# 1/rms of a stage's input norm multiplied in behind the products, on an eight-stage kernel

## The reference

```python
def rms_norm(x, g):
    y = x * lax.rsqrt(jnp.mean(x * x, axis=-1, keepdims=True) + EPS)
    return y * g
mixer_a: u, v, z = split(h @ w_in); v = rms_norm(v, v_gain); mixed = causal w_s over chunks of 128 (v) + b_s
         y = u * mixed * silu(z);  return y @ w_out
mixer_b: q, k, v for 3 dilated window patterns x 8 heads: rms_norm of q and k, rotary, windowed softmax, merge of the three
         y = o * silu(z);  return y @ w_out
mixer_c: xc, z = split(h @ w_in); pooled = causal means of xc over 2, 4, 8, 16
         y = ((pooled - xc) @ w_grp) * scale * silu(z);  return y @ w_out
swiglu:  (silu(h @ w_gate) * (h @ w_up)) @ w_down
even mixer: differential attention (4 heads) | u * sigmoid(gate) -> causal convolution of 31 taps -> layernorm -> silu;  @ w_out
odd mixer:  S5 state space recurrence on 256 channels | latent attention (6 heads) with norms of both latents;  @ w_out
```

## Time and profile before

| what | value |
|---|---|
| median of 3 runs | 3223.59 us (3222.73 to 3223.64) |
| profiled execution, span | 3221.1 us |
| PE busy | 3003.4 us, 93% |
| DVE busy | 1588.9 us, 49% |
| ACT busy | 1105.8 us, 34% |
| POOL busy | 322.8 us, 10% |

### The profile page before, as it was taken

How to read it: one execution, slowest core, us unless ns; L and a number is a source line. 1 busy time by engine, 2 the same in 40 slices (tenths; PEclk the granted TensorE clock), 3 DMA queues, 4 the chain that set the end, 5 groups by cost and what they waited for, 6 DMA issues and landing times.

```text
span 3221.1 us, 37674 instructions
## 1 busy us (share of the span) xinstructions
PE 3003.4 (93%) x13472; PEld 2403.3 (75%) x13472; DVE 1588.9 (49%) x2188; ACT 1105.8 (34%) x1575; POOL 322.8 (10%) x281
## 2 busy tenths in 40 slices
PE   7999999998999899998999988689999888889998
PEld 6888787877788777776888866467888654668886
DVE  5444444553355454454444487844333578453333
ACT  3332223452344432223332244434222333442222
POOL 1000001100111000000000042210000443000001
PEclk9999999999999999999999988789999898999999
DMA  3222221112111122222222221012222210112222
GB/s 137 99 91 91 99 92 59 53 53 73 66 59 53 59 93 91 86 92 79 92 91 93 90 79 53 20 67 86 97 98 98 81 51 13 59 63 100 92 97 85
DMA packets 69245, 252.04 MB, mean 78 GB/s; under 512 B 7680, under 2 KB 7680, under 8 KB 68480
## 3 DMA queue, kind: packets, MB, share of 16 engines
q1 hardware_dynamic: 66960, 241.89, 22.2%
q10 hardware_dynamic: 2160, 8.49, 0.7%
HBM read 248.25 MB, written 2.10 MB: 78 GB/s over the span
## 4 chain that ended last, share of the span: by engine, by line
PE 81%; DVE 11%; issue 3%; ACT 3%; POOL 2%; DMA 0%; ACTq 0%; POOLq 0%; DVEq 0%
PE ps L276 18%; PE ps L278 18%; PE ps L277 18%; PE ps L492 2%; PE ps L493 2%; PE ps L494 2%; DVE arena L1549 2%; PE ps L702 1%; PE ps L665 1%; PE ps L666 1%; PE ps L667 1%; PE ps L712 1%; PE ps L692 1%; PE ps L510 1%; PE ps L1002 1%
## 5 line engine op out<-in xcount | busy, mean ns | idle before, releaser
L265 DVE TENSOR_TENSOR w_low<-raw,w_high 128x1024 fp32r<-128x1024 f32 x456 | 577.5, 1269 | 533.9 <-ACT w_high L258 524.8
L276 PE MATMUL ps<-h_high,w_high 128*128 128x512 f32 x1968 | 785.4, 399 | 27.9 <-DVE h_low L379 26.0
L277 PE MATMUL ps<-h_low,w_high 128*128 128x512 f32 x1968 | 772.6, 393 | 0.0
L278 PE MATMUL ps<-h_high,w_low 128*128 128x512 f32 x1968 | 772.1, 392 | 0.0
L258 ACT ACTIVATE w_high<-raw 128x1024 fp32r<-128x1024 f32 x456 | 478.0, 1052 | 467.9 <-PE ps L278 233.9
L276 PEld LDWEIGHTS ps<-h_high,w_high 128*128 128x128 f32 x1968 | 372.6, 189 | 121.6 <-issue 32.1
L278 PEld LDWEIGHTS ps<-h_high,w_low 128*128 128x128 f32 x1968 | 372.9, 189 | 78.4
L277 PEld LDWEIGHTS ps<-h_low,w_high 128*128 128x128 f32 x1968 | 373.4, 190 | 74.5 <-issue 1.4
L276 PE MATMUL ps<-y_high,w_high 128*128 128x512 f32 x800 | 313.9, 392 | 0.5 <-DVE y_low L1456 0.4
L277 PE MATMUL ps<-y_low,w_high 128*128 128x512 f32 x800 | 312.7, 391 | 0.0
L278 PE MATMUL ps<-y_high,w_low 128*128 128x512 f32 x800 | 312.5, 391 | 0.0
(11 more groups left out here) (343 smaller groups left out, 3950.7 us busy)
## 6 DMA issues: line engine op xcount, KB each, us to landing
raw<-stream SPq DMA_DIRECT2D x456, 512.0 KB, 3.2
table<-tables_in ACTq DMA_DIRECT2D x5, 1088.0 KB, 5.0
x<-x_in ACTq DMA_DIRECT2D x8, 256.0 KB, 8.2
x_out<-x SPq DMA_DIRECT2D x8, 256.0 KB, 2.0
const<-const_in SPq DMA_DIRECT2D x1, 673.0 KB, 4.9
work<-ssm_in ACTq DMA_DIRECT2D x1, 512.0 KB, 3.7
params<-params_in ACTq DMA_DIRECT2D x1, 287.0 KB, 8.6
```

Source lines behind the costliest of these rows:

```text
L265: nc.vector.tensor_tensor(w_low[:, u.slot], raw[:, u.raw], w_high[:, u.slot].bitcast(F32), ALU.subtract).then_inc(weights_low, 1)
L276: nc.tensor.matmul(bank, wh, high[:, k], start=k == 0, stop=False)
L277: nc.tensor.matmul(bank, wh, low[:, k], start=False, stop=False)
L278: mm = nc.tensor.matmul(bank, wl, high[:, k], start=False, stop=k == tiles - 1)
```

## The change

The split input of a stage no longer holds 1/rms: `h_high` and `h_low` are the split of x * gain. They are made tile by tile by `high_of` (ACT) and `low_of` (DVE) as the output products of the stage before are added to x (argument `following`), or in the post norm's pass. The column sums stand behind the first unit of the next stage (in b ahead of its first product), the spread in the middle of its second (`mid`), and ACT copies 1/rms to SBUF (`late_keep`). In b it is spread near the end of each half. Wherever a product leaves PSUM, DVE multiplies it by 1/rms: u, z in a; x tiles and z in c; gate and up in f; gates, and the rotary tables, in e; the inputs of the recurrence and the rotary key in o; v and z in b. So silu and sigmoid read SBUF behind that multiply, and PE's waits for a bank are for DVE's take (`c_z_taken`, `f_gate_taken`, `b_z_taken`) and no longer for ACT. The epsilons of inner norms are scaled (`norm_eps`, `b_args`, `o_args`). In the post norm's pass DVE adds all tiles; POOL adds the squares, as for the other norms, and the sums by ones and the reciprocal of a full tile are gone. `normalise()` goes. At the start the raw loads are issued ahead of const, and params right behind the first x tile.

```diff
+        def high_of(act, name, k):
+            xk, gain, high, _ = h_tile(name, k)
+            nc.scalar.activation(high, xk, ACT.Copy, scale=gain).then_inc(h_high_done, 1)
+        def low_of(dve, name, k):
+            xk, gain, high, low = h_tile(name, k)
+            dve.wait_ge(h_high_done, 8 * H_NO[name] + k + 1)
+            nc.vector.scalar_tensor_tensor(out=low, in0=xk, scalar=gain, in1=high.bitcast(F32), op0=ALU.mult,
+                                           op1=ALU.subtract).then_inc(h_low_done, 1)
+        def norm_sums(pe, r, classes=False):
+            if r > 0:
+                pe.wait_ge(norm_added, r)
+            pe.wait_ge(norm_gathered, 6 * (r + 1))
+            column_sums(root, 0, classes).then_inc(norm_summed, 1)
+            pe.wait_ge(norm_squared, 8 * (r + 1))
+            column_sums(ssq, 1, classes).then_inc(norm_summed, 1)
+        def late_keep(act, name, bank, target):
+            act.wait_ge(late_spread, S_NO[name] + 1)
+            nc.scalar.activation(target, ps[:, bank], ACT.Copy).then_inc(late_kept, 1)
...
                     u = Unit(first + at + j, loop, per)
                     split_low(dve, u + AHEAD)
+                    if following is not None and at + j > 0:
+                        low_of(dve, following, at + j - 1)
                     dve.wait_ge(units_done, u.count(1))
...
         def b_tensor(pe, t, first, o, y_base, r, last=False, following=None):
             pe.wait_ge(out_free, 8 * o + 2)
+            norm_sums(pe, R_PRE["b"], True)
...
+                    if (j, u) == (BH, 1):
+                        pe.wait_ge(b_k_done, lin(3 * BH, i, 3 * BH))
+                        norm_spread(pe, R_PRE["b"], 3).then_inc(b_r_spread, 1)
...
-                            pe.wait_ge(b_silu, lin(u - 1, i, BH))
+                            pe.wait_ge(b_z_taken, lin(u - 1, i, BH))
                         product(pe, unit, ps[:, n % 2], h_high, h_low)
...
-                    if j == BH and u < 3:
-                        dve.wait_ge(b_o_copied, lin(u + 1, i, 3))
-                        gate(u, b_o[:, u])
+                    if j == BH and 1 <= u <= BH:
+                        m = u - 1
+                        dve.wait_ge(b_r_kept, lin(1, i, 1))
+                        dve.wait_ge(units_done, b_unit(first, i, BH, m).count(1))
+                        nc.vector.tensor_tensor(b_szs[m % 2][:], ps[:, m % 2], b_r[:], ALU.mult).then_inc(b_z_taken, 1)
+                        if m < BH - 1:
+                            dve.wait_ge(b_o_copied, lin(m + 1, i, 3))
+                            gate(m, b_o[:, m])
...
             for k in range(KD):
                 if k >= 2:
-                    dve.wait_ge(*post_done(p, k - 2))
+                    dve.wait_ge(post_added, 8 * p + k - 1)
                 nc.vector.scalar_tensor_tensor(out=full[:, k % 2], in0=source[:, k], scalar=par(gain, k), in1=ps[:, 7],
                                                op0=ALU.mult, op1=ALU.mult).then_inc(post_scaled, 1)
-                if k % 2:
+                if k >= 1:
                     add(k - 1)
+                if k >= 2 and following is not None:
+                    low_of(dve, following, k - 2)
...
                     split_low(dve, Unit(plan[g][0] + m + AHEAD))
+                    if g == 0 and m == 0:
+                        norm_rstd(dve, R_PRE["c"])
+                        dve.wait_ge(late_kept, S_NO["c"] + 1)
                     dve.wait_ge(units_done, plan[g][0] + m + 1)
...
+                    nc.vector.tensor_tensor(c_x[:, b], ps[:, m], rstd[:], ALU.mult).then_inc(c_pool, 1)
...
+                    dve.wait_ge(units_done, plan[g][1] + m + 1)
+                    nc.vector.tensor_tensor(c_sz[:, m], ps[:, 4 + m % 2], rstd[:], ALU.mult).then_inc(c_z_taken, 1)
...
+                if slot > 0 and e_unit(slot - 1)[1] == "b" and slot % 2 == 0:
+                    m = e_unit(slot - 1)[2]
+                    dve.wait_ge(e_sig, m + 1)
+                    dve.wait_ge(e_taken, e_takes(m) + 2)
+                    nc.vector.tensor_tensor(e_u[:, m, PADT:], e_u[:, m, PADT:], e_sg[m % 2][:], ALU.mult).then_inc(e_gated, 1)
...
-            pool.wait_ge(rstd_spread, R_PRE["o"] + 1)
+            pool.wait_ge(norm_summed, 2 * (R_PRE["o"] + 1))
             nc.gpsimd.tensor_copy(o_eb, early).then_inc(o_small_done, 1)
...
-            sp.dma_start(const[:], const_in).then_inc(const_loaded, 16)
             for s in range(RAW_SLOTS):
                 sp.dma_start(raw[:, s], stream[s]).then_inc(weights_loaded[s], 16)
+            sp.dma_start(const[:], const_in).then_inc(const_loaded, 16)
```

More of the change, by code:

```diff
@@ L266, in split_low, with product @@
                                     ALU.subtract).then_inc(weights_low, 1)
-        def product(pe, u, bank, high, low, ready=None, tiles=KD):
+        def product(pe, u, bank, high, low, ready=None, tiles=KD, mid=None):
             pe.wait_ge(weights_low, u.count(1))
             for k in range(tiles):
+                if mid is not None and k == tiles // 2:
+                    mid()
                 if ready is not None:
@@ new lines, in norm_sums, with norm_spread @@
+        def norm_sums(pe, r, classes=False):
[5 more added lines that the diff above has]
+            column_sums(ssq, 1, classes).then_inc(norm_summed, 1)
+        def norm_spread(pe, r, bank):
+            pe.wait_ge(rstd_done, r + 1)
+            for b in range(NBLK):
+                mm = nc.tensor.matmul(ps[:, bank, b * P:(b + 1) * P], norm_rstds[:, b:b + 1].to_broadcast([P, P]), ident,
@@ L349, in norm_rstd @@
[L349 to L364 removed]
+            act.wait_ge(norm_added, r + 1)
@@ L409, in rounds, with out_product @@
                     body(i, 0)
-        def out_product(pe, o, first, y_base, tiles=KD, r=None, last=False):
+        def out_product(pe, o, first, y_base, tiles=KD, r=None, last=False, following=None):
             def body(loop, at):
@@ L419, in out_product, with out_split @@
             rounds(pe, last, body)
-            if r is not None:
-                norm_sum(pe, r)
-        def out_split(act, o, first, target=None, r=None, last=False):
+            if r is not None and following is None:
+                norm_sums(pe, r)
+                norm_spread(pe, r, 7).then_inc(rstd_spread, 1)
+        def out_split(act, o, first, target=None, r=None, last=False, following=None):
             def body(loop, at):
@@ L512, in a_tensor, with a_scalar @@
                         mm.then_inc(mix_done, 1)
[L513 to L515 removed]
+                out_product(pe, o + half, start + 16, y_base + 8 * half, r=r if half == 1 else None, last=last and half == 1,
+                            following=following)
+        def a_scalar(act, a, t, first, o, y_base, r, last=False, following=None):
+            name = A_NAMES[a]
             for c in range(4):
@@ L588, in a_vector_part @@
                                                 ALU.subtract).then_inc(y_low_done, 1)
-                out_take(dve, o + half, start + 16, x, r=r if half == 1 else None, last=last and half == 1)
+                out_take(dve, o + half, start + 16, x, r=r if half == 1 else None, last=last and half == 1,
+                         following=following if half == 1 else None)
         BH = 4
@@ L2350, in _ @@
                     f_tensor(pe, AGAIN[name], H_NO[name], FIRST[name], O_NO[name], Y_BASE[name], r, last)
-                if name in P_NO and not last:
-                    norm_sum(pe, r + 1)
         @block.gpsimd
@@ L2368, in _ @@
                     norm_gather(pool, r)
-                if name in P_NO:
-                    post_gpsimd(pool, P_NO[name])
+                if name in P_NO and not last:
+                    norm_gather(pool, r + 1)
 def stream_b(w_in, w_out):
```

517 lines of the change are left out of this document (285 added, 232 removed).

## The result

The changed kernel takes 3243.3 us (3238.8 to 3245.5, 4 runs) against 3223.6 for the kernel before: ratio 1.0060, 95% interval 1.0046 to 1.0075. That is 19.7 us slower, where 15.5 were forecast. The profiled execution has a span of 3241.5 us, 20.4 over that of before.

What follows compares the result with a forecast made beforehand. PE was taken as the bound. Boundaries -29, start -7.5, f0 and f1 -2.5 each, o +5.5, b +27 and +2, c +13, e +8.5, the rest +0.5 twice: +15.5 on 3223.6, so 3239 us, range 3215 to 3257.

Steps and rivals of the forecast that it cites:

- the start and the four boundaries: Kernel start, -7.5 us, and the pre norms of b, c, a1 and e without a post norm, -29 us.
- a0 to b: Boundary ahead of b: everything behind the column sums goes, 5 us, with some 1 us of slow clock: -6.
- b's ends: End of both b halves: z's take stands behind the softmax on DVE, 13.5 us a half: +27, bounds +18 and +32.
- e: Stage e: extra multiplies, and the gate's product behind the next slot's split and softmax, about 6.3 and 2: +8.5 us.
- b to c: Boundary ahead of c: gain of 9.9 us partly given back, third z product waiting 3 to 4: -6.
- c's groups: Stage c: 2.9 us longer before each of three groups, plus 1.5 of low clock: +13, bounds +9 and +17.
- The reading of the round as DVE's own: Stage c: an x tile is a DVE round of 5.74 us, and each gets one more multiply, 0.73 with its gap.
- Post passes: Behind e, f0 and o: -2.5 us for f0, +5.5 for o with its recurrence later, -2.5 for f1.
- The third rival: Post passes: each POOL addition costs DVE 0.93 us, not 0.4, adding 9.5: 3248.5 us, chance 0.13.
- The first (b hidden): Rival: at b's end the wait for the take is hidden, both halves costing 3 us: 3215 us, chance 0.17.
- The second (losses even out): Rival: clock doesn't fall in c's and b's new gaps; b 18, c 9, e 4: 3221.5 us, chance 0.20.
- The fourth (2 us more behind each new gap): Rival: low clock behind each of some 10 new gaps costs 2.0 us more: 3259 us, chance 0.10.

Runs made afterwards that it cites:

- kernel 1: Changed kernel with b's multiply of z by 1/rms, and ACT's copy of 1/rms, moved ahead of the softmax and exp: 3225.1 us.
- kernel 2: Changed kernel with 20 dummy matmuls before PE's wait for b's third and fourth z product: 3240.6 us.
- Kernel 5: Changed kernel with b's column sums moved ahead of PE's wait for the last addition to x: 3236.9 us.
- Kernels 3, 6 and 7: Changed kernel with c's low part on POOL (3251.7 us); with that and ACT's split ahead of its copy (3232.1); with ACT's split move alone (3235.2).
- kernel 4: Changed kernel with e's gate banks handed back by the multiplies with 1/rms instead of the gate's product: 3238.5 us.
- kernel 8: Changed kernel with POOL's additions of squares in the three post passes cut to 16 of 512 columns, norms wrong: 3222.1 us.
- kernel 11: Changed kernel with the post passes' squares summed on PE in the next stage's first unit, not added on POOL: 3248.1 us.

## Why the prediction was right, and where it was off

**The sign and the size.** Slower by 19.7 where 15.5 were forecast. The norms' path became shorter by 32.9 us in the start and the four boundaries (36.7 forecast), and the multiplies put in behind PSUM cost more than that: 30.1 in b, 11.5 in c, 4.3 in e. That the total came so near is in part luck: a0 to b missed by 4.9 us, b's ends and f1 by 3.1 each, and e by 4.2 to the other side.

**b's ends.** The step was right: the third and fourth z product wait for a take that stands behind a softmax; the gaps are 5.12 us (4.4 + 0.7 = 5.1 in the sum), and kernel 1 removes them. The softmaxes lie 15.6 and 16.0 us apart, not 12.7 and 14: the product behind each gap is lengthened by the low clock, which the sum holds apart. That term was undersized: 9.3 us by kernel 2, where the sum had 7 to 8 in its 27.

**a0 to b.** The step that failed is "all behind them goes: -6". Measured is -1.1. The prediction let the sums run where and as they ran before. But they now stand behind PE's wait for the last addition, and as their weights lie four columns apart they take 2.0 us each and not 1.0. They end 3.4 us later (388.54 + 2.00 + 7.7 = 398.2 for 394.84). The rest is the low clock: the prediction let 1 us of slow matmuls go with the gap, and there are 2.1 us of them in b's first unit where there were 1.5. Kernel 5 gives 2.3 back, half of it slow matmuls. What adjacent columns would give was not tried.

**b to c** gave 5.7 for 6: the third z product waited 2.99 us, as forecast (3), and slow matmuls behind it cost 1.7.

**c's groups.** The gap of 5.34 is the forecast 2.37 + 2.9 = 5.3. The low clock behind it was forecast at 1.5 us for each group; it came as 1.3 behind the third gap and 1.6 in the last output units, and behind the first two it had been there before. The reading of the round as DVE's own was wrong: its length came out right only because the multiply lies on the part of the ring that is DVE's, which was luck. Kernels 3, 6 and 7 showed that.

**e** cost 4.3 for 8.5. The mechanism is shown by kernel 4. PE's waits hold one wait for a gate's product, of 6.2 us (6.3 in the sum), and not the second of 2. Why less than its length was lost is not shown.

**Post passes.** -2.8, +6.0 and +0.6 for -2.5, +5.5 and -2.5. The third rival, contention, is shown as a mechanism by kernel 8: beside POOL the last h_low of a pass comes 5.0 us later (20.8 for 15.8), where the sum had 2.4 and the rival 5.6, and PE's wait for POOL's last addition comes on top. (The rival's 0.93 for each addition is a slip: the earlier trace rows give 1.796 - 0.752 = 1.04.) The sum came near all the same, because it took the pass without POOL at 17 us and more, and it takes 15.8. The Trainium skill (GPSIMD Engine Reference, Specifications) names contention with POOL for DVE instructions that have two SBUF inputs; here the traces agree, for `low_of` and the additions to x, where they start while POOL adds (last section). The addition in the pass of the kernel before was not lengthened: all 12 of them start 0.16 us ahead of POOL's.

**The other rivals.** The first (b hidden) fell with the trace. The second (losses even out) is excluded by the interval. The fourth (2 us more behind each new gap) held behind b's gaps and behind c's third z product, and in c's groups behind one gap of three. That DVE is 112 us busier does not matter as such: in a and f, where each output tile has more DVE work, the two traces keep their distance to 1 us from the second unit to the output products.

## What to carry to other kernels

Moving a factor behind the products takes it off a serial path once per stage, but it moves the release of every PSUM bank to the engine that multiplies, and there to the place in its queue where the multiply stands. Price each such take by what stands ahead of it, and place it as early as its operands allow: in b that alone gave back 18 of the 20 us. Where a loop's round passes over two engines, find the ring before moving an operation off one of them.

## What the hardware showed that was not expected

**The clock behind a pass comes in two ways.** The same code behind a post norm, in kernels whose edits lie elsewhere, starts its second unit 24.8 or 26.0 us into the pass, and its third at 31.2 or at 34.6 to 35.3 (f0 and f1). In the changed kernel's trace f0 had the one and f1 the other, a difference of 3.6 us with nothing changed. The kernel before had 34.5 in both. Other places vary too: the first units come 1.3 to 2.9 us later in 8 of the 12 traces than in the changed kernel's, and stage e took up to 2.9 us more with the same code. Together they may be what spreads the runs of the changed kernel over 7 us, and it is why gains of 3 to 5 us were read in the traces by place and not from medians.

**Operations on DVE beside POOL.** `low_of` took 1.76 or 0.74, the addition 0.68, 1.10 or 1.76, of the same shape in the same loop. It goes by who starts first. In the three passes of the changed kernel 18 such operations with two SBUF inputs start while POOL adds, and each ends 0.55 us behind the end of POOL's addition: with 1.21 us of it left the operation takes 1.76, with 0.55 left 1.10. The nine additions that start 0.11 us ahead of POOL's keep their 0.68, and POOL's then takes 1.70, where its other ones in the pass take 1.46. DVE's first operation on a tile, with one SBUF input and one from PSUM, keeps its 0.73 in either case. Mean ns of a line hide this: 923 for an addition that is 680, 1100 or 1760.

**Column sums** of 4 matmuls with one column took 0.95 to 1.05 us at a granted clock of 1.00 and 1.70 at 0.50 (kernel 11): small matmuls pay for the low clock as large ones do. With weights four columns apart the first sum behind a0 took 1.8 (kernel 5) to 2.03 at 1.00.
